# Differential attention with scaled queries, negated maxima and joint ratios, and moved casts in the first norm

## What is computed

```python
q = q.reshape(B, T, H, 2, d) * (d ** -0.5)
s = jnp.einsum('bqhjd,bshjd->bhjqs', q, k).astype(jnp.float32)
p = jax.nn.softmax(s, axis=-1)
a = (p[:, :, 0] - lam_full * p[:, :, 1]).astype(v.dtype)
o = jnp.einsum('bhqs,bshe->bqhe', a, v)
return _rms(o) * subln_g * (1.0 - lam_init)
```

## Time and profile before

| | |
|---|---|
| median of 3 runs | 1944.27 us (1944.01 to 1947.92) |
| the profiled execution | 1947.03 us |
| its span, first to last instruction | 1945.4 us |
| TensorE busy | 1898.2 us (98%) |
| VectorE busy | 1142.9 us (59%) |
| ScalarE busy | 666.0 us (34%) |
| POOL busy | 136.2 us (7%) |
| mean granted TensorE clock | 0.989 |
| DMA moved | 269.75 MB |

### The profile page before, as it was taken

How to read it: one execution, slowest core, us unless ns; L and a number is a source line. 1 busy time by engine, 2 the same in 40 slices (tenths; PEclk the granted TensorE clock), 3 DMA queues, 4 the chain that set the end, 5 groups by cost and what they waited for, 6 DMA issues and landing times.

```text
span 1945.4 us, 29214 instructions
## 1 busy us (share of the span) xinstructions
PE 1898.2 (98%) x10896; PEld 1663.5 (86%) x10896; DVE 1142.9 (59%) x1858; ACT 666.0 (34%) x1052; POOL 136.2 (7%) x196
## 2 busy tenths in 40 slices
PE   7999999999989999999999999999999999999998
PEld 6888888898965798888889888888898998999998
DVE  6877772264468468777523877753262534755554
ACT  4332222242247333222222423222243422544442
POOL 0010000100001211101010101000100000010000
PEclk9999999999999899999999999999999999999999
DMA  8466643334210036666332566633343320545554
GB/s 313 140 205 193 195 153 91 104 118 148 87 44 1 23 103 208 196 195 195 109 101 91 180 193 196 195 119 101 95 143 120 102 93 13 178 156 172 183 163 131
DMA packets 80861, 269.75 MB, mean 139 GB/s; under 512 B 8977, under 2 KB 14353, under 8 KB 80785
## 3 DMA queue, kind: packets, MB, share of 16 engines
q1 hardware_dynamic: 62354, 201.58, 32.0%
q0 software_dynamic: 18432, 67.12, 11.3%
HBM read 267.62 MB, written 1.05 MB: 138 GB/s over the span
## 4 chain that ended last, share of the span: by engine, by line
PE 91%; DVE 5%; issue 1%; ACT 1%; POOL 0%; POOLq 0%; DVEq 0%; ACTq 0%
PE pt L1265 23%; PE pt L1268 23%; PE pt L1266 23%; PE pt L1365 3%; PE pt L1475 2%; PE pt L1474 2%; PE pt L1476 2%; PE pt L1612 2%; PE pt L1614 2%; PE pt L1613 2%; PE pt L1558 1%; PE pt L1369 1%; PE pt L1491 1%; PE pt L1510 1%; DVE wl L774 1%
## 5 line engine op out<-in xcount | busy, mean ns | idle before, releaser
L774 DVE TENSOR_TENSOR wl<-raw,wh 128x1024 fp32r<-128x1024 f32 (+2 forms) x394 | 432.2, 1136 | 517.1 <-ACT wh L542 513.0
L1265 PE MATMUL pt<-xh,wh 128*128 128x512 f32 (+1 forms) x1632 | 585.5, 359 | 0.1
L1266 PE MATMUL pt<-xh,wl 128*128 128x512 f32 (+1 forms) x1632 | 584.8, 358 | 0.0
L1268 PE MATMUL pt<-xl,wh 128*128 128x512 f32 (+1 forms) x1632 | 583.1, 358 | 0.0
L542 ACT CAST wh<-raw 128x1024 fp32r<-128x1024 f32 (+2 forms) x394 | 364.0, 971 | 243.0 <-PE pt L1268 184.1
L1266 PEld LDWEIGHTS pt<-xh,wl 128*128 128x128 f32 x1632 | 309.0, 189 | 45.2
L1265 PEld LDWEIGHTS pt<-xh,wh 128*128 128x128 f32 x1632 | 309.0, 189 | 45.0 <-issue 0.3
L1268 PEld LDWEIGHTS pt<-xl,wh 128*128 128x128 f32 x1632 | 308.7, 189 | 45.0
L786 DVE CUSTOM_DVE_ANT_0 pt<-modw,raw 128x1024 f32<-128x1024 f32 x256 | 305.5, 1252 | 4.5 <-DMA modw<-in_mod_rows 4.2
L1265 PE MATMUL pt<-uh,wh 128*128 128x512 f32 (+1 forms) x572 | 203.9, 356 | 0.0
L1266 PE MATMUL pt<-uh,wl 128*128 128x512 f32 (+1 forms) x572 | 203.9, 356 | 0.0
(11 more groups left out here) (186 smaller groups left out, 2312.5 us busy)
## 6 DMA issues: line engine op xcount, KB each, us to landing
raw<-in_ffn_w SPq DMA_DIRECT2D x238, 512.0 KB, 4.0
modw<-in_mod_rows POOLq DMA_DIRECT2D x128, 512.0 KB, 4.6
raw<-in_ret_w_in SPq DMA_DIRECT2D x48, 512.0 KB, 4.7
raw<-in_diff_w_in SPq DMA_DIRECT2D x24, 512.0 KB, 4.2
raw<-in_ffn_w SPq DMA_DIRECT2D x32, 256.0 KB, 3.9
raw<-in_ret_w_out SPq DMA_DIRECT2D x16, 512.0 KB, 4.1
region<-in_mod_rows SPq DMA_DIRECT2D x8, 512.0 KB, 14.4
region<-in_mod_start SPq DMA_DIRECT2D x8, 512.0 KB, 14.9
```

The source lines that it names most:

```text
L774: nc.vector.tensor_tensor(flat(wl[:, s, cut]), raw[:, raw_slot(late, s, p), 0:part_rows * CW], flat(wh[:, s, cut].bitcast(F32)), ALU.subtr ...
L1265: nc.tensor.matmul(bank, w_hi[:, k, cut], hi(k), start=a, stop=False)
L1266: nc.tensor.matmul(bank, w_lo[:, k, cut], hi(k), start=False, stop=False)
L1268: return nc.tensor.matmul(bank, w_hi[:, k, cut], lo(k), start=False, stop=b)
```

## The change

Six edits. The queries are multiplied by 1/8 when ScalarE copies them out of PSUM, with an activation in the place of a copy for queries and keys and for the copies of the retention that share the helper. The exponentials then have no factor. The row maximum is written negated by the reduction itself, into `shift`, and the product behind it is gone, with its semaphore. The reciprocal and the ratio are made for both row blocks of a unit together, at the odd steps, and both mixings follow them. In the first norm ScalarE casts the second pieces behind tile 2 and the two parts of `extra_hi` behind tiles 6 and 7; VectorE subtracts these parts behind the remainders of tiles 6 and 7. A doubled wait of POOL is gone.

```diff
@@ gpsimd
-                    if u0 == START_UNITS:
-
-                        pool.wait_ge(lo_ready, 4)
@@ scalar: copy_out
-            def copy_out(ph, dst, T, i, s):
+            def copy_out(ph, dst, T, i, s, factor=1.0):
...
-                    nc.scalar.copy(row(dst, 4 * i + 2 * s + t)[:, 0:T], pt[:, 2 * s + t, 0:T]).then_inc(evac[s], 1)
+                    nc.scalar.activation(row(dst, 4 * i + 2 * s + t)[:, 0:T], pt[:, 2 * s + t, 0:T], ACT.Copy,
+                                         scale=factor).then_inc(evac[s], 1)
@@ scalar: first norm
-                            if k == 3:
+                            if k == 2:
                                 start_pieces(1)
-                            if k == 5:
-
-                                for p in range(2):
-                                    act.wait_ge(raw_landed[p], 16 * raw_count(False, 1, 0))
-                                    nc.scalar.copy(flat(extra_hi[:, p * DT // 2:(p + 1) * DT // 2]), raw[:, p, :]).then_inc(hi_ready, 1)
+                            if k >= DT - 2:
+
+                                p = k - (DT - 2)
+                                act.wait_ge(raw_landed[p], 16 * raw_count(False, 1, 0))
+                                nc.scalar.copy(flat(extra_hi[:, p * DT // 2:(p + 1) * DT // 2]), raw[:, p, :]).then_inc(hi_ready, 1)
@@ scalar: diff_qk and ret_k
-                    with act.Fori(0, (2 if kind != "diff_qk" else 4)) as i:
+                    if kind == "diff_qk":
+
+                        with act.Fori(0, 2) as i:
+                            for s in range(2):
+                                copy_out(ph, dst, T, i, s, factor=DD ** -0.5)
+                    with act.Fori(2 if kind == "diff_qk" else 0, 4 if kind == "diff_qk" else 2) as i:
@@ scalar: exps
-                            nc.scalar.activation(ex(u, b)[:, j, 0:nk], pt[:, 2 * b + j, 0:nk], ACT.Exp, scale=DD ** -0.5,
+                            nc.scalar.activation(ex(u, b)[:, j, 0:nk], pt[:, 2 * b + j, 0:nk], ACT.Exp,
@@ vector: first norm
+                    def extra_rest(p):
+                        half = slice(p * DT // 2, (p + 1) * DT // 2)
+                        dve.wait_ge(hi_ready, 5 + p)
+                        nc.vector.tensor_tensor(flat(extra_lo[:, half]), raw[:, p, :], flat(extra_hi[:, half].bitcast(F32)),
+                                                ALU.subtract).then_inc(lo_ready, 1)
...
-                        if k == 6:
-                            for p in range(2):
-                                half = slice(p * DT // 2, (p + 1) * DT // 2)
-                                dve.wait_ge(hi_ready, 5 + p)
-                                nc.vector.tensor_tensor(flat(extra_lo[:, half]), raw[:, p, :], flat(extra_hi[:, half].bitcast(F32)),
-                                                        ALU.subtract).then_inc(lo_ready, 1)
                         if k + 1 < DT:
                             start_products(k + 1)
                         if k + 2 < DT:
                             start_tile(k + 2)
+                        if k == DT - 1:
+                            extra_rest(0)
                     start_lo(DT - 1)
+                    extra_rest(1)
@@ vector: attention
-                        nc.vector.tensor_reduce(top[:, 2 * b:2 * b + 2], pt[:, 2 * b:2 * b + 2, 0:nk], AX.X, ALU.max).then_inc(topped, 1)
-                        dve.wait_ge(topped, 2 * u + b + 1)
-                        nc.vector.tensor_scalar(shift[:, 2 * b:2 * b + 2], top[:, 2 * b:2 * b + 2], -(DD ** -0.5), None,
-                                                ALU.mult).then_inc(shifted, 1)
+                        nc.vector.tensor_reduce(shift[:, 2 * b:2 * b + 2], pt[:, 2 * b:2 * b + 2, 0:nk], AX.X, ALU.max,
+                                                negate=True).then_inc(shifted, 1)
+                    def ratios(u):
+
+                        dve.wait_ge(exped, 4 * u + 4)
+                        if u:
+                            dve.wait_ge(mixed, 2 * u)
+                        m = mass[:, 8 * (u // 2 % 2) + 4 * (u % 2):8 * (u // 2 % 2) + 4 * (u % 2) + 4]
+                        nc.vector.reciprocal(ratio[:, 2:4], m[:, 1:4:2]).then_inc(ratio_ready, 1)
+                        dve.wait_ge(ratio_ready, 2 * u + 1)
+                        nc.vector.scalar_tensor_tensor(ratio[:, 0:2], m[:, 0:4:2], neglam, ratio[:, 2:4], ALU.mult,
+                                                       ALU.mult).then_inc(ratio_ready, 1)
+                        dve.wait_ge(ratio_ready, 2 * u + 2)
                     def mix(u, b):
                         nk = TOK if u % 2 == 0 else CTX
-                        v = 2 * u + b
-                        dve.wait_ge(exped, 2 * v + 2)
...
                         nc.vector.scalar_tensor_tensor(e[:, 0, 0:nk], e[:, 1, 0:nk], ratio[:, b:b + 1],
                                                        e[:, 0, 0:nk], ALU.mult, ALU.add).then_inc(mixed, 1)
@@ vector: the loop over v
-                            mix(v // 2, v % 2)
+                            if v % 2:
+                                ratios(v // 2)
+                                for b in range(2):
+                                    mix(v // 2, b)
```

More of the change, by code:

```diff
@@ L296, in trunk @@
                                                    sem("roped"))
-        scored, topped, shifted, exped = sem("scored"), sem("topped"), sem("shifted"), sem("exped")
+        scored, shifted, exped = sem("scored"), sem("shifted"), sem("exped")
         ratio_ready, mixed, probs_turned, probs_ready = (sem("ratio_ready"), sem("mixed"), sem("probs_turned"),
@@ L1138, in row_max @@
                         dve.wait_ge(scored, 2 * u + b + 1)
-                        nc.vector.tensor_reduce(top[:, 2 * b:2 * b + 2], pt[:, 2 * b:2 * b + 2, 0:nk], AX.X, ALU.max).then_inc(topped, 1)
-                        dve.wait_ge(topped, 2 * u + b + 1)
-                        nc.vector.tensor_scalar(shift[:, 2 * b:2 * b + 2], top[:, 2 * b:2 * b + 2], -(DD ** -0.5), None,
-                                                ALU.mult).then_inc(shifted, 1)
+                        nc.vector.tensor_reduce(shift[:, 2 * b:2 * b + 2], pt[:, 2 * b:2 * b + 2, 0:nk], AX.X, ALU.max,
[10 more added lines that the diff above has]
+                        dve.wait_ge(ratio_ready, 2 * u + 2)
                     def mix(u, b):
                         nk = TOK if u % 2 == 0 else CTX
-                        v = 2 * u + b
-                        dve.wait_ge(exped, 2 * v + 2)
[L1148 to L1155, removed]
+                        e = ex(u, b)
                         nc.vector.scalar_tensor_tensor(e[:, 0, 0:nk], e[:, 1, 0:nk], ratio[:, b:b + 1],
```

## The result

The changed kernel takes 1979.93 us (median of 4 runs, 1978.61 to 1981.25), the one before 1944.42 in the same comparison: a ratio of 1.0176, with a 95% interval of 1.0160 to 1.0191 (the plain quotient of the two medians is 1.0183, inside it). It is 35.5 us slower. The profiled execution took 1981.25 us, its span is 1979.5.

The account below looks back on a forecast made before the run. TensorE was taken as the bound, busy 98% of the span, with VectorE nearly as full in the attention. From 1947.0 us, +24 + 6 - 6.3 gave 1970.7, or 1968 for the median; range 1958 to 1982.

Parts of the forecast that it names:

- The chain: Attention: score, maximum, ratio, mixing and transpose run serially, 14.2 us a head instead of 11.0; +24 us in all.
- the ramp and the last head: Attention's ends, where steps are missing and others wait: 1 to 3 us more, beside 22 for seven intervals.
- The clock: Attention: pauses bring six more stretches at 1.2 GHz, 1.1 us each, +6 us; ends 0 and 14.
- The first norm: Start of the kernel: earlier casts shorten TensorE's wait, extra tile at 60.4 instead of 66.74 us; gain 6.3 us.
- if the clock then stays up: First norm: condition for each further tile after TensorE's earlier start to cost 4.55 us.
- The copies: ScalarE's scaled copies as activations cost nothing on the path; without idle cover, 16 at some 0.1 us, 2 us.
- the negated maximum: VectorE in the attention: price bounded between 0 and 0.17 us, taken as 0.
- the lost product: Attention: dropping the small product after each row maximum frees VectorE of 0.19 us a block.
- VectorE's gain: Attention: lost products and joint reciprocals and ratios give VectorE back 1.7 us a head.
- Saved work wins: Rival, attention: VectorE's savings go into TensorE's pauses, at most 10 us; with the norm, 1928 us; chance 0.06.
- Late but not queued: Rival, attention: only block 1's exponentials delay block 0, a head of 12.0 us, total 1946, no change; chance 0.05.
- The clock low throughout: Rival: clock stays at 1.2 GHz through the attention, +7 us a head, 56 instead of 6, total 2018; chance 0.05.

Follow-up runs that it names:

- e3_norm_only: Only the first norm's moved casts and remainders, put into the kernel before: 1941.12 us, ratio 0.9969.
- e6_pieces_only: Only ScalarE's casts of the second pieces moved behind tile 2, in the kernel before: 1940.75 us, ratio 0.9966.
- e1_single_mix: The changed kernel with reciprocal, ratio and mixing by row block again, all else as changed: 1933.5 us, ratio 0.9933.
- e9_behind_filler: Changed kernel, next unit's block 0 row maximum behind the mixings, three unread matmuls before each even unit's first mixing wait: 1953.42 us, ratio 1.0036.

## Why the prediction was right, and where it was off

The sign, the mechanism and the range held: 1979.9 lies in 1958 to 1982, close to its upper end, and the forecast of 1968 was 12 us short: some 8 of them are the clock, 2 the first norm in this execution, the rest small terms.

**The chain** was sized at 14.2 us a head from the rows of the kernel before; the one undisturbed interval is 14.15:

```profile
589.44 0.17 DVE L1152 RECIPROCAL small<-small 128x2 f32<-128x2 f32 x1 [0.26 <-ACT region L712]
...
590.71 0.66 PE L1410 MATMUL pt<-keep,region 128*128 128x128 f32 x4 [2.27 <-DVE region L1160]
...
596.59 0.16 DVE L1152 RECIPROCAL small<-small 128x2 f32<-128x2 f32 x1
...
597.58 0.44 PE L1410 MATMUL pt<-keep,modw 128*128 128x128 f32 x2 [2.18 <-DVE modw L1160]
```

The next even reciprocal is at 603.59. So the halves are 7.15 and 7.00 us, where the sum had 7.14 and 7.02, with two pauses of about 2.2 us, both ended by a mixing. In the even unit the reciprocal waits for the exponentials, in the odd one for the maximum, as the two halves of the chain had it. Over the seven intervals, 14.15 us each would be 99.1 where the kernel before took 77.4, its own stretches at 1.2 GHz with them: 21.6 more, of 22 forecast; the ramp and the last head took 2.9 more, of 1 to 3. The runs give the parts: 10.59 by row block, about 12.7 with the maxima behind the mixings (an estimate, 12.91 measured with fillers), 14.15 with the maximum ahead. Moving the maximum out of the way thus gives back 1.5 of the 3.6 us that the joint ratios cost. The other 2.1 are not lateness alone, since in that order the maxima wait for the mixings.

**The clock** is the term that was mis-sized. I put 1.1 us on each of six more stretches, 6 us; the seven intervals took 113.1 us, 14.0 beyond their 99.1, and the stage has 14.6 us beyond the 24 of the chain. The mean granted clock over it fell from 0.91 to 0.81, that is from some 19 to some 54 us at 1.2 GHz. Two things were wrong: several stretches were longer than the 3.4 us of the one in the earlier trace rows (13.6 us from 555.1 on, 6.8 us from 572.2, 650.7 and 667.7 on), and a stretch cost more here, 1.3 to 1.6 us in the three heads of mean clock 0.88 or 0.89 where it was 1.1 in the earlier trace rows. That TensorE's steps now all stand in the chain would explain this; it was not tried by itself. My upper end for the term, 14, is what came. The page of the Trainium skill, "TensorE: Matmul & The Clock Gate", section "Why this matters for your kernels", by which pauses this short would leave the clock alone, would have given 1962. The trace disagrees: no pause in the stage was over 3.0 us, none from 590 us to the last score over 2.3, and each of the four heads from 604 us on had a stretch at 1.2 GHz all the same. It was right not to go by it.

**The first norm** gave 4.1 of the 6.3 us in the profiled execution. The pause shrank as worked out; the step that did not hold there is "if the clock then stays up": it fell for 3.4 us all the same, 1.6 us on one tile, and the timeline ran 0.4 us later before the edit took effect. In four other executions the clock did stay up, and the extra tile started at 60.4 to 61.4 us, as forecast; the totals of e3_norm_only and e6_pieces_only, 6.5 and 6.2 us, are in line with 6.3. The sum went by one of two outcomes, and nothing in its rows could tell which would come.

**The copies, the negated maximum and the lost product** cost nothing that shows, and e1_single_mix has the expected head. The copies of L561 took 532 ns each and take 543 as activations, where a tenth of a microsecond more was feared. VectorE's gain was 1.7 us a head by start times; in busy time, which leaves out the gaps between small operations, it is 1.2. A slip of 0.02 us is in its working (603.69 less 603.48 is 0.21, not 0.19); nothing hangs on it. **Saved work wins** fell: VectorE was relieved by 1.2 us a head and the head grew by 3.1. The page "Perfetto Trace Analysis" of the Trainium skill, section "Optimizing Scalar/DVE Operations", which favours grouping on a saturated engine, says further down that breaking up instructions may help where an engine is not saturated but makes others wait; in this stage VectorE was at 86% and the second sentence was the one that held (10.59 against 14.15 us). **Late but not queued** was put at a head of 12.0 us and no change. e9_behind_filler, the nearest to it, has 12.91, of which some 0.2 are fillers, and 1.0036: it loses less than the changed kernel, and still loses. **The clock low throughout** did not come: it recovered in every head.

## What to carry to other kernels

When two small operations are joined on an in-order engine, list what stands between the first one's old place and the new one: here a row maximum whose input came from the engine that was waiting, and the saving of 1.2 us a head bought a serial chain of 3.1. Price such a chain by adding the durations of one period from the trace, which came out to 0.05 us, and then add the clock's reaction to the new pauses as a term of its own, here more than half of the first. Look at more than one execution before a few microseconds are put down to the clock: behind one and the same pause it fell in some and not in others. A cast that another engine waits for belongs as early in its engine's idle time as its input allows.

## What was not expected of the hardware

TensorE's granted clock was at 1.2 GHz for 24 of the 31 us between 555 and 586 us, where pauses of TensorE were 2 to 3 us each with work in between; three extra matmuls ahead of each unit's first wait kept it at 2.4 GHz from the first score to the last and made a kernel with more work 13 to 15 us faster. Behind one pause of 0.6 us in the first norm it fell for 3.4 us in five executions and not at all in four; the changed kernel, where it fell, and e1_single_mix, where it did not, have the same instructions there. The reciprocal and the ratio on two columns took as long as on one (0.17 and 0.22 us), and the negated row maximum as long as the plain one (1.23 us).
